# Three-pass mixer projections in layer 0 of a two-block network, and token tiles summed, scaled and turned in two halves between its expert layers

## The chip, the cores and the metric

The kernel runs on one core of a Trainium2 chip. The metric is the time of one execution on the device in microseconds, the median of several runs.

The engines of the core are named as the profile names them. PE is TensorE (matmuls), and PEld its weight loads. DVE is VectorE, ACT is ScalarE, POOL is GpSimd. SP issues most DMAs. Each engine works through its own queue in order, and the kernel orders the engines among each other by semaphores written out by hand.

## The reference

Two blocks of two layers each follow one another on 256 tokens of width 1024. The first block (an mLSTM and neighbourhood attention, then a differential attention, each with memory attention and a gated feed-forward part) is not touched by the change except at its seam with the second block. The second block is:

```python
def layer(x, xc, ..., need_ctx):
    h = rms_norm_2(x, n1) * (1 + sc1) + sh1
    hc = rms_norm_2(xc, n1) * (1 + csc1) + csh1
    a_b, a_c, a_h, b_v, b_g, c_q, c_k, c_v, d_q, d_k, d_v = split_proj(h @ w_in)
    ca_b, ca_c, ca_h, ... , cd_v = split_proj(hc @ w_in)
    ya = short_conv_mixer(a_b, a_c, a_h, conv_a)
    yb = conformer_conv(b_v, b_g, conv_b, ...)          # 31 taps over the tokens
    yc = window_attention(apply_rope(c_q), apply_rope(c_k), c_v, ...)
    yd = global_attention(apply_rope(rms(d_q)), apply_rope(rms(d_k)), d_v, ...)
    x_new = x + g1 * (concatenate([ya, yb, yc, yd]) @ w_out)
    h2 = rms_norm_2(x_new, n2) * (1 + sc2) + sh2
    x_new = x_new + g2 * expert_choice_ffn(h2, router, w_gate, w_up, w_down)
    ...                                                 # the same for xc where need_ctx
```

In layer 0 the 256 tokens x and the 256 context tokens xc both go through all of it; in layer 1 only x does, and xc gives keys and values alone. Each layer has 16 experts with three matrices of 1024x1024 in float32, all of which are read from HBM: some 200 MB per layer.

## The kernel before, in words

**Stages.** The first block takes the first 1020 us or so. Then come, for layer 0 of the second block: the projections by `w_in` (columns in five blocks, in the order b, d, c, ab, ah of `IN2_BLOCKS`), the 31-tap convolution and the norms and rotations of queries and keys beside them, the attention of 16 units, the output projection by `w_out`, the routing, and the experts in 8 groups of two. Layer 1 follows with the same stages for half the tokens, with 4 groups of four experts.

**Two ways to multiply.** In the first block the weights are *split*: ACT rounds a unit (128 partitions x 4 chunks x 512 columns, 1 MB) into one of four slots for high parts (`split_through`, L1733), POOL subtracts that from the whole unit in place, chunk by chunk, which leaves the low part (L1638, `w_lo`), and PE multiplies in three passes, high by high, low by high and high by low (`passes`, L624 to L626), with both operands as fp32r. A high slot is free again when PE has read the unit four before it; POOL walks through all the units in one loop (L1630 and after), in which a few waits, `yields`, are written in. In the second block the operands are plain float32, and each float32 matmul stands in the trace as two records. The `w_in` units of the second block are loaded straight into slots of the ring of 12.

**Layer 0, projections.** PE first multiplies the context half of the four outputs of block b (L1149), while DVE finishes the last norm of the first block, then turns the token rows (L1165), then multiplies the token half. ACT and DVE share the evacuation of the turned rows, which scales and shifts them (L2124, L2750). Blocks d and c have two outputs of queries (L1198, by halves of 64 columns), one of keys (L1189) and one of values, made with the tokens in the partitions (L1206). Block ab has four outputs and ah two (L1189). The ah outputs are computed behind the first two units of the attention.

**Beside them.** DVE computes the gate of the convolution (L2766), then its 31 taps for two channel halves (L2771, L2773: 60 operations of one tap), then root and rotation of queries and keys (L2794, L2800, L2802, L2781 to L2784), then the norm of the convolution's rows (L2810 to L2819), then the maxima of the attention (L2385 to L2398). PE waits for it at the rotation of dk0 (L1224), before the first scores (L824) and at each turning of probabilities (L836). POOL computes gate diagonals and small tables (L1667 to L1691) and is then idle until the short convolution (L1699).

**Between the layers.** The last group's outputs are scattered by 8 matmuls into 8 banks (L1451) and added to x by DVE (L2964) in the order of `sums_of`, in which context and token tiles alternate. ACT squares each tile (L2091), DVE scales it (L2957), and PE turns all four tiles (L1177) before the first output of block b.

**DMA.** SP issues the loads in the order of use. Each waits until the slot it overwrites has been read. The first 19 quarter matrices of layer 0's experts have homes of their own; the rest follow in the ring as PE reads it.

Of the kernel before, what the change touches and what calls it, by code (L numbers as in the profile page):

```python
# [219 lines left out]
def build(nc, w, out, table, stop=None):  # L220
    marks = Marks(table)
    units = weight_plan(w)
    first2 = [key[0] for key, _ in units].index("in2")
# [21 lines left out]
    with ExitStack() as ctx:  # L245
# [69 lines left out]
        x_lo, m_lo = xT_r[:, :, 0:SEQ], xT_r[:, :, SEQ:2 * SEQ]  # L315
        y1_lo = x_r[:, 2:4, :].rearrange("p a (b c) -> p (a b) c", c=SEQ)
# [77 lines left out]
        last_sum_banks = (6, 7, 0, 1, 2, 3, 4, 5)  # L394
# [165 lines left out]
        QK_AT = dict(cq0=0, cq1=1, ck0=2, dq0=4, dq1=5, dk0=6)  # L560
        ROT_BANK = dict(cq0=6, cq1=7, ck0=6, dq0=7, dq1=4, dk0=5)
# [9 lines left out]
        def _(pe):  # L571
# [544 lines left out]
            for layer in range(DEPTH):  # L1116
# [27 lines left out]
                def chunk_half(name, b, wb, at, s, first):  # L1144

                    for c in range(KC):
                        if not first and name == "bv0" and c % 2 == 0:
                            pe.wait_ge(*after("hT_odd" if c // 2 % 2 else "hT", (layer, 0, c // 2)))
                        mm = pe.matmul(b[:, SEQ * s:SEQ * s + SEQ], wb(c)[:, at:at + P], xT[:, c, SEQ * s:SEQ * s + SEQ],  # L1149
                                       start=(first and c == 0), stop=(not first and c == KC - 1))  # L1150
                    return mm

                if layer == 0:
                    wb0 = w_block(("in2", layer, "b"))
                    early = [(name, at, open_bank(("c", layer, name), 4 + i)) for i, (name, at) in enumerate((k, v) for k, v in CHUNKS.items() if k[0] == "b")]
                    pe.wait_ge(*after("hT_odd", "ctx"))
                    for name, at, b in early:
                        chunk_half(name, b, wb0, at - IN2_BLOCKS[0][1], 1, True)
                    for t in range(T2):
                        pe.wait_ge(*after("xhat", (layer, 0, t)))  # L1160
                    for j in range(4):
                        b = dense_bank(("h", layer, 0, j))
                        for c in (2 * j, 2 * j + 1):
                            for t in range(T2):
                                mm = pe.transpose(b[:, 256 * (c % 2) + P * t:256 * (c % 2) + P * t + P], xhat[:, t, P * c:P * c + P], ident)  # L1165
                        mm.then_inc(*filled_now(("h", layer, 0, j)))
                    for name, at, b in early:
                        chunk_half(name, b, wb0, at - IN2_BLOCKS[0][1], 0, False)\
                            .then_inc(bank_full[fills[("c", layer, name)][0]], 1)
                        last_fill[0] = full(("c", layer, name))  # L1170
                else:
                    for t in range(4):
                        pe.wait_ge(*after("xhat", (layer, 0, t)))
                    for c in range(KC):
                        b = dense_bank(("h", layer, 0, c))
                        for t in range(4):
                            mm = pe.transpose(b[:, P * t:P * t + P], xhat[:, t, P * c:P * c + P], ident)  # L1177
                        mm.then_inc(*filled_now(("h", layer, 0, c)))
                def chunk_there(c):

                    pe.wait_ge(*after("hT_odd" if c % 2 else "hT", (layer, 0, c)))

                def chunk(name, wb, at, n=n_tok):
                    key = ("c", layer, name)
                    b = open_bank(key, LATE_BANK[name]) if name in LATE_BANK else dense_bank(key)
                    for c in range(KC):
                        if layer and name == "bv0":
                            chunk_there(c)
                        mm = pe.matmul(b[:, 0:n], wb(c)[:, at:at + P], xT[:, c, 0:n], start=(c == 0), stop=(c == KC - 1))  # L1189
                    mm.then_inc(*filled_now(("c", layer, name)))  # L1190

                def queries(name, wb, j):

                    b = dense_bank(("c", layer, name))
                    for c in range(KC):
                        for v in range(2):
                            at = HD * (2 * v + j)
                            mm = pe.matmul(b[HD * v:HD * v + HD, 0:n_tok], wb(c)[:, at:at + HD], xT[:, c, 0:n_tok],  # L1198
                                           start=(c == 0), stop=(c == KC - 1))
                    mm.then_inc(*filled_now(("c", layer, name)))  # L1200

                def values2(name, wb, at):
# [5 lines left out]
                    mm.then_inc(*filled_now(("c", layer, name)))  # L1208

# [29 lines left out]
                for blk, n0, n1 in IN2_BLOCKS:  # L1239
                    wb = wb0 if (layer, blk) == (0, "b") else w_block(("in2", layer, blk))  # L1240
                    if blk in "dc":
                        for i in range(2):
                            queries(f"{blk}q{i}", wb, i)
                        if blk == "c":
                            square_sums2(("dq0", "dq1"))
                        chunk(blk + "k0", wb, 2 * P, 2 * SEQ)
                        values2(blk + "v", wb, 3 * P)
                        if blk == "c":
                            square_sums2(("dk0",))
                            rotations(("cq0", "cq1"))  # L1250
                        if blk == "d":
# [10 lines left out]
                            mm.then_inc(*filled_now(("refold", layer)))  # L1262
# [1857 lines left out]
```

## Time and profile before

| | |
|---|---|
| median of 3 runs | 2422.28 us (2420.02 to 2424.28) |
| the profiled execution | 2422.65 us, its span on the core 2420.8 us |
| PE busy | 2184.5 us (90%) |
| PEld busy | 1350.8 us |
| DVE busy | 752.7 us |
| ACT busy | 633.9 us |
| POOL busy | 740.4 us |
| mean granted TensorE clock | 0.961 of full speed |
| HBM read | 633.17 MB |

The shares of the whole span hide that the stages differ. The first block and layer 0's mixer are full of PE work; the expert stages run at 407 to 428 GB/s of DMA. The change touches the stretch from about 1020 us to 1310 us (layer 0 without its experts) and the seam at 1765 us to 1860 us, so the profile is to be read there.

### The profile page before, as it was taken

The numbers are of one execution on the slowest core, as the hardware profiler recorded it, in microseconds if no ns is written. First come the engines' busy times: TensorE is split into PE (matmuls) and PEld (weight loads), VectorE is DVE, ScalarE is ACT, GpSimd is POOL, SyncE is SP. The second block draws the span as 40 slices with busy tenths as digits, with TensorE's granted clock in tenths as the row PEclk, the third lists the DMA queues.
The fourth block names the chain that finished last, engine by engine and source line by source line (L and its number), as shares of the span: only waits on it lengthen the run. The fifth ranks groups of instructions, "written<-read, shape, count | busy, mean of one in ns | idle before, by whom it ended". The sixth has DMA issues, their size and how long they took to land.

```text
span 2420.8 us, 32870 instructions
## 1 busy us (share of the span) xinstructions
PE 2184.5 (90%) x13382; PEld 1350.8 (56%) x13382; DVE 752.7 (31%) x1440; ACT 633.9 (26%) x925; POOL 740.4 (31%) x624
## 2 busy tenths in 40 slices
PE   7998999999799999999999999999889995888885
PEld 7876789878687898865543333333257642222221
DVE  4864220122622212377623222222147420010101
ACT  3544333444544334112512000010022420000001
POOL 7665367897183777710300000000010200000000
PEclk9999999999899999999999999999999998999998
DMA  9433759755157697441215899999962369999997
GB/s 299 140 120 125 261 198 325 236 183 174 36 187 252 209 324 238 149 173 38 84 52 209 347 428 428 429 429 429 423 226 83 127 279 424 427 428 428 429 428 306
DMA packets 151381, 635.98 MB, mean 263 GB/s; under 512 B 7816, under 2 KB 14216, under 8 KB 120920
## 3 DMA queue, kind: packets, MB, share of 16 engines
q1 hardware_dynamic: 148224, 623.78, 66.3%
q0 software_dynamic: 2608, 9.25, 1.4%
q8 instruction: 86, 1.41, 0.2%
q10 hardware_dynamic: 424, 1.22, 0.1%
q14 instruction: 39, 0.32, 0.0%
HBM read 633.17 MB, written 1.05 MB: 262 GB/s over the span
## 4 chain that ended last, share of the span: by engine, by line
PE 65%; DMA 19%; DVE 7%; POOL 4%; ACT 2%; issue 2%; SPq 1%; DVEq 0%; ACTq 0%; POOLq 0%
PE bank L1374 14%; PE bank L624 9%; PE bank L626 9%; PE bank L625 9%; DMA ring<-in_w_gate 8%; DMA ring<-in_w_up 7%; DMA ring<-in_w_down 4%; PE bank L1189 4%; PE bank L1332 3%; POOL ring_r L1638 2%; PE bank L847 2%; PE bank L970 2%; PE bank L1198 2%; PE bank L824 1%; PE bank L1206 1%
## 5 line engine op out<-in xcount | busy, mean ns | idle before, releaser
L1374 PE MATMUL bank<-ring,arena 128*32 128x512 f32 x4424 | 651.5, 625 | 127.0 <-DMA ring<-in_w_gate 54.6
L1638 POOL TENSOR_TENSOR ring_r<-ring,ring_r 128x512 fp32r<-128x512 f32 (+1 forms) x468 | 574.9, 1270 | 294.1 <-ACT ring_r L1733 265.1
L1374 PEld LDWEIGHTS bank<-ring,arena 128*32 128x32 f32 x4424 | 191.5, 114 | 562.3 <-issue 536.4
L624 PE MATMUL bank<-ring_r 128*128 128x256 f32 (+1 forms) x1504 | 463.5, 308 | 13.0 <-POOL ring_r L1638 7.8
L626 PE MATMUL bank<-xT_r,ring_r 128*128 128x256 f32 x1248 | 354.3, 284 | 0.0
L625 PE MATMUL bank<-ring_r 128*128 128x256 f32 x1104 | 312.4, 283 | 0.0
L624 PEld LDWEIGHTS bank<-ring_r 128*128 128x128 f32 x1504 | 289.3, 192 | 35.9 <-issue 16.7
L1733 ACT ACTIVATE ring_r<-ring 128x2048 fp32r<-128x2048 f32 (+1 forms) x119 | 216.7, 1827 | 288.7 <-DMA ring<-in_ffn_w_gu 139.9
L626 PEld LDWEIGHTS bank<-xT_r,ring_r 128*128 128x128 f32 x1248 | 239.6, 192 | 0.0
L625 PEld LDWEIGHTS bank<-ring_r 128*128 128x128 f32 x1104 | 211.6, 192 | 0.7 <-issue 0.5
L1667 POOL TENSOR_TENSOR arena<-const 128x1024 f32<-128x1024 f32 x6 | 12.0, 2002 | 592.0 <-DVEq L2284 522.6
L1765 ACT ACTIVATE arena<-bank 128x512 f32<-128x512 f32 (+1 forms) x144 | 83.6, 581 | 257.1 <-PE bank L836 72.0
L2252 ACT ACTIVATE arena<-bank 128x512 f32<-128x512 f32 x24 | 13.0, 594 | 486.6 <-PE bank L1374 486.6
L2964 DVE TENSOR_TENSOR x<-x,bank 128x512 f32<-128x512 f32 x80 | 52.0, 684 | 218.3 <-PE bank L1451 217.7
L1189 PE MATMUL bank<-xT,ring 128*128 128x512 f32 (+1 forms) x320 | 110.7, 504 | 1.9 <-ACTq L2200 1.9
L1638 POOL TENSOR_TENSOR spare_r<-spare,ring_r 128x512 fp32r<-128x512 f32 x76 | 100.5, 1360 | 12.0 <-ACT ring_r L1733 7.2
L1189 PEld LDWEIGHTS bank<-xT,ring 128*128 128x128 f32 x320 | 63.0, 199 | 44.7 <-issue 37.1
L2939 DVE TENSOR_TENSOR arena<-bank,arena 128x512 f32<-128x512 f32 x24 | 15.5, 686 | 232.6 <-PE bank L1374 232.6
L626 PE MATMUL bank<-ring_r 128*128 128x512 f32 x208 | 84.3, 405 | 0.0
L624 PE MATMUL bank<-ring_r,arena_r 128*128 128x512 f32 (+1 forms) x208 | 79.3, 381 | 2.2 <-POOL ring_r L1638 2.0
L1699 POOL TENSOR_TENSOR arena<-arena 128x512 f32<-128x512 f32 (+1 forms) x4 | 3.8, 950 | 250.6 <-ACTq L1771 250.4
L625 PE MATMUL bank<-ring_r,arena_r 128*128 128x512 f32 (+1 forms) x208 | 78.5, 378 | 0.0
(358 smaller groups left out, 2719.6 us busy)
## 6 DMA issues: line engine op xcount, KB each, us to landing
ring<-in_w_gate SPq DMA_DIRECT2D x52, 2048.0 KB, 17.3
ring<-in_w_up SPq DMA_DIRECT2D x52, 2048.0 KB, 17.3
ring<-in_w_down SPq DMA_DIRECT2D x40, 2048.0 KB, 18.2
ring<-in_ada_w SPq DMA_DIRECT2D x41, 1024.0 KB, 7.5
ring<-in_w_down SPq DMA_DIRECT2D x41, 1024.0 KB, 18.4
ring<-in_ffn_w_gu SPq DMA_DIRECT2D x35, 1024.0 KB, 5.7
ring<-in_w_up SPq DMA_DIRECT2D x18, 1024.0 KB, 8.7
ring<-in_w_gate SPq DMA_DIRECT2D x17, 1024.0 KB, 5.0
```

Source lines behind the costliest of these rows:

```text
L624: pe.matmul(dst, w_hi, v_hi, start=first, stop=False)
L625: pe.matmul(dst, w_lo, v_hi, start=False, stop=False)
L626: return pe.matmul(dst, w_hi, v_lo, start=False, stop=last)
L847: mm = pe.matmul(b[p0:p0 + dv, 256 * i:256 * i + 256], u["v"][kb][:, i * dv:(i + 1) * dv], probsT_of(u)[:, kb, :], start=(kb == 0), stop=( ...
L970: mm = pe.matmul(b[32 * j:32 * j + 32, :], scT[:, UK * h + k, :], ws[j][:, k], start=(h == 0 and k == 0), stop=(h == 1 and k == UK - 1))
L1189: mm = pe.matmul(b[:, 0:n], wb(c)[:, at:at + P], xT[:, c, 0:n], start=(c == 0), stop=(c == KC - 1))
L1332: mm = pe.matmul(b[:, :], src[:, t * P:t * P + P], wb(c), start=(c == 0), stop=(c == KC - 1))
L1374: mm = pe.matmul(dst[nb][CAP * b:CAP * b + CAP, :], src[:, c, CAP * b:CAP * b + CAP], rooms[b % G], start=bi_first, stop=bi_last)
L1638: pool.tensor_tensor(lo[:, c], whole[:, c], hi_of(u)[:, c, 0:n], ALU.subtract).then_inc(*signal("w_lo", (u, c)))
L1733: act.activation(hi_of(u)[:, 0:kc, 0:n_col], room_of(slot)[:, 0:kc, 0:n_col], ACT.Copy).then_inc(*signal("w_hi", u))
L1765: link(act.activation(dst, src, func))
L2964: dve.tensor_tensor(xs, xs, bank[bank_at][:, :], ALU.add).then_inc(m["sum_free"], 1)
```

## The change

- The `w_in` units of layer 0 join the split units: they are loaded into the slots of raw units, rounded by ACT and subtracted by POOL. The ring begins with the `w_out` units of layer 0, whose first two slots hold the high parts of the layer's input (`h_hi`) until block ah has been multiplied.
- The input of layer 0's projections is split too. DVE scales the turned context in PSUM, copies the high part and subtracts the low part; for the tokens ACT writes the high part, and DVE scales in PSUM and subtracts.
- All outputs of blocks b, d, c, ab, ah of layer 0 are made by three passes (`split_chunk`). The values are made turned, like the others, and then turned back by PE (`turn_values`). The queries' columns are put in order when the inputs are prepared, so that one output has 128 columns, in both layers.
- ACT's splits for block d stand after the norm's root, for c after the sigmoids, for ab after the evacuation of dv, for ah after that of cv. POOL does block b's subtractions before, and the other eight units' after, its small tables.
- Between the layers the two token tiles are summed, scaled and turned first (`turn_hidden(0)`), and the two context tiles follow (`turn_hidden(1)`, before block d). The banks of the last sums change.

```diff
-    first2 = [key[0] for key, _ in units].index("in2")
+    first2 = [key[0] for key, _ in units].index("out2")
...
+        h_hi, h_lo = ring_r[:, MEM_HI:X_HI + 1].rearrange("p s a b -> p (s a b)").rearrange("p (c n) -> p c n", c=KC), xT_r
...
-        last_sum_banks = (6, 7, 0, 1, 2, 3, 4, 5)
+        last_sum_banks = (0, 4, 1, 5, 2, 6, 3, 7)
...
+                def split_chunk(name, wb, at, wait=False):
+
+                    key = ("c", layer, name)
+                    b = open_bank(key, LATE_BANK[name]) if name in LATE_BANK else dense_bank(key)
                     for c in range(KC):
+                        mm = passes(b[:, :], wb(c, at, wait), (h_hi[:, c], h_lo[:, c]), c == 0, c == KC - 1)
+                    mm.then_inc(*filled_now(key))
...
+                    turn_hidden(0)
+                    for c in range(KC):
+                        if c % 2 == 0:
+                            pe.wait_ge(*after("hT_odd", (layer, 0, c // 2)))
+                        for name, at, b in early:
+                            mm = passes(b[:, 0:SEQ], wb0(c, at - IN2_BLOCKS[0][1], False), (h_hi[:, c, 0:SEQ], h_lo[:, c, 0:SEQ]), False, c == KC - 1)
...
+                def turn_values(name):
+
+                    pe.wait_ge(*after("proj", ("vT", name)))
+                    b = dense_bank(("vt", name))
+                    for t in range(4):
+                        mm = pe.transpose(b[:, P * t:P * t + P], qk[:, VT_AT[name], P * t:P * t + P], ident)
+                    mm.then_inc(*filled_now(("vt", name)))
...
                         if blk == "c":
                             square_sums2(("dk0",))
                             rotations(("cq0", "cq1"))
+                            if layer == 0:
+                                turn_values("cv")
...
+            in2_at = place[unit_at[("in2", 0, "b", 0)]]
+            lows(0, in2_at + 2)
...
                 ins.then_inc(*signal("spread", layer))
+                if layer == 0:
+                    lows(in2_at + 2, len(split_units))
...
                     norm_rows(0, range(T2))
+                    split_through(place[unit_at[("in2", 0, "d", 1)]])
...
+                if layer == 0:
+                    split_through(place[unit_at[("in2", 0, "c", 1)]])
...
-                evac(("c", layer, "dv"), v2[:, :, 1, :])
+                values_in("dv")
+                if layer == 0:
+                    split_through(place[unit_at[("in2", 0, "ab", 1)]])
...
-                evac(("c", layer, "cv"), v2[:, :, 0, :])
+                values_in("cv")
+                if layer == 0:
+                    split_through(place[unit_at[("in2", 0, "ah", 1)]])
+                roots(("dk0",))
...
-                        mean_of(ready[1])
-                        scaled_rows(ready[0])
-                        mean_of(ready[2])
-                        scaled_rows(ready[1])
-                        mean_of(ready[3])
-                        scaled_rows(ready[2])
-                        scaled_rows(ready[3])
+                        mean_of(0)
+                        add_half(2, 0)
+                        mean_of(1)
+                        scaled_rows(0)
+                        scaled_rows(1)
+                        add_half(2, 1)
+                        for nb in range(2):
+                            add_half(3, nb)
+                        mean_of(2)
+                        mean_of(3)
+                        scaled_rows(2)
+                        scaled_rows(3)
```

## Rows read from the trace of the kernel before

**Rows 1.** Stages: us, busy time (instructions) of PE, PEld, DVE, ACT, POOL, clock, DMA

```profile
1050.00:1100.00 50.00, 50.00 (x237) 23.76 (x234) 46.90 (x63) 9.58 (x18) 0.00 (x0) 1.00 0.24 85
1151.00:1223.00 72.00, 68.18 (x296) 40.01 (x294) 44.56 (x120) 39.64 (x96) 20.03 (x14) 1.00 0.17 65
1309.00:1765.00 456.00, 422.90 (x3440) 139.74 (x3444) 89.86 (x171) 39.56 (x62) 0.00 (x0) 0.97 0.96 407
```

**Rows 2.** Timeline of PE in layer 0: start us, us, engine, line, operation, count

```profile
1019.90 13.97 PE L1149 MATMUL bank<-xT,ring 128*128 128x256 f32 x64
1033.71 1.91 PE L1165 MATMUL bank<-const,arena 128*128 128x128 f32 x16
1098.09 7.03 PE L1189 MATMUL bank<-xT,ring 128*128 128x512 f32 x16
1130.25 3.72 PE L824 MATMUL bank<-arena 64*128 64x256 f32 x16
1150.62 1.09 PE L836 MATMUL bank<-const,arena 128*128 128x128 f32 x8
```

**Rows 3.** Timeline of PE, three-pass products of the first block, 512 and 256 wide

```profile
984.33 0.40 PE L626 MATMUL bank<-ring_r,arena_r 128*128 128x512 f32 x1
985.03 0.40 PE L626 MATMUL bank<-ring_r,arena_r 128*128 128x512 f32 x1
...
904.81 0.28 PE L624 MATMUL bank<-ring_r 128*128 128x256 f32 x1
905.16 0.28 PE L624 MATMUL bank<-ring_r 128*128 128x256 f32 x1
```

**Rows 4.** Timeline of DVE in layer 0

```profile
1015.98 0.70 DVE L2322 SCALAR_TENSOR_TENSOR bank<-x,bank 128x512 f32<-128x512 f32 x1 [20.41 <-PE bank L626]
1029.42 2.73 DVE L2732 TENSOR_SCALAR arena<-x,rstd 128x1024 f32<-128x1024 f32 x2
1051.38 0.55 DVE L2771 TENSOR_SCALAR arena<-arena,cols 128x512 f32<-128x512 f32 x1 [0.15 <-DVE arena L2766]
1076.29 23.59 DVE L2773 SCALAR_TENSOR_TENSOR arena<-arena,cols 128x512 f32<-128x512 f32 x30
1127.69 0.42 DVE L2784 TENSOR_TENSOR arena<-arena 128x256 f32<-128x256 f32 x1
1142.70 0.88 DVE L2408 TENSOR_SCALAR arena<-arena,small 128x512 f32<-128x512 f32 x2
```

**Rows 5.** Timeline of ACT and POOL: splitting, the turned tokens, a table load

```profile
994.90 1.92 ACT L1733 ACTIVATE ring_r<-ring 128x2048 fp32r<-128x2048 f32 x1 [5.02 <-PE bank L626]
...
992.21 17.54 POOL L1638 TENSOR_TENSOR ring_r<-ring,ring_r 128x512 fp32r<-128x512 f32 x14
...
1034.41 1.02 ACT L2124 ACTIVATE xT<-bank,const,gain 128x256 f32<-128x256 f32 x2 [5.23 <-PE bank L1165]
1043.58 1.28 ACT L2135 ACT_TABLE_LOAD   x1 [0.17 <-ACT arena L1765]
```

**Rows 6.** First block, DVE beside POOL: a group of 41:54 us, then timeline rows

```profile
L2493 DVE SCALAR_TENSOR_TENSOR arena<-arena,cols 128x256 f32<-128x256 f32 x1 | 14.5, 14516 | 0.0
...
...
78.11 1.64 DVE L2474 TENSOR_TENSOR arena<-arena,x 4x512 f32<-4x512 f32 x1
74.48 6.68 POOL L1638 TENSOR_TENSOR ring_r<-ring,ring_r 128x512 fp32r<-128x512 f32 x4
```

**Rows 7.** Timeline of SP's loads for layer 0's experts

```profile
1171.79 0.43 SPq L1527 DMA_DIRECT2D spare<-in_w_down  x1
1230.15 0.33 SPq L1527 DMA_DIRECT2D arena<-in_w_gate  x1
```

**Rows 8.** Timeline of PE at the seam and in layer 1

```profile
1780.14 6.30 PE L1177 MATMUL bank<-const,arena 128*128 128x128 f32 x32 [8.68 <-DVE arena L2957]
...
1847.50 3.62 PE L1189 MATMUL bank<-xT,ring 128*128 128x256 f32 x16
1856.55 5.30 PE L1189 MATMUL bank<-xT,ring 128*128 128x256 f32 x16
```

More of the change, by code:

```diff
@@ L1142, in gate_slots, with split_block, chunk_of @@
                             keep_busy(2)
-                def chunk_half(name, b, wb, at, s, first):
-                    for c in range(KC):
[L1147 to L1151, printed above, removed]
+                def split_block(key):
+                    parts = [split_weights(key, h) for h in range(2)]
+                    def chunk_of(c, at, wait):
+                        u, hi, lo = parts[c // UK]
+                        if wait:
+                            chunk_split(u, c % UK)
+                        return hi[:, c % UK, at:at + P], lo[:, c % UK, at:at + P]
+                    return chunk_of
@@ L1183, in chunk, with chunk_there @@
+                    read(("in2", layer, "b"), 2)
+                else:
+                    turn_hidden(0)
+                def chunk_there(c, s):
+                    if c % 2 == 0:
+                        pe.wait_ge(*after("hT_odd" if c // 2 % 2 else "hT", (layer, s, c // 2)))
                 def chunk(name, wb, at, n=n_tok):
@@ L1186, in chunk @@
                     for c in range(KC):
-                        if layer and name == "bv0":
-                            chunk_there(c)
+                        if layer and name in ("bv0", "dk0"):
+                            chunk_there(c, 1 if name == "dk0" else 0)
                         mm = pe.matmul(b[:, 0:n], wb(c)[:, at:at + P], xT[:, c, 0:n], start=(c == 0), stop=(c == KC - 1))
[L1190 to L1199, printed above, removed]
                     mm.then_inc(*filled_now(("c", layer, name)))
@@ L1262, in _ @@
                             mm.then_inc(*filled_now(("refold", layer)))
+                            if layer == 0:
+                                turn_values("dv")
                     elif blk == "ab":
-                        chunk("ab0", wb, 0)
+                        gated = chunk if layer else split_chunk
+                        if layer:
+                            chunk("ab0", wb, 0)
+                        else:
+                            split_chunk("ab0", wb, 0, wait=True)
                         rotations(("ck0", "dq0", "dq1"))
@@ L1272, in _ @@
                             scores(u)
[L1273 to L1275 removed]
+                        gated("ac0", wb, 2 * P)
+                        gated("ac1", wb, 3 * P)
+                        read(("in2", layer, "ab"), 2)
+                    elif blk == "b":
                         for name, at in CHUNKS.items():
@@ L1648, in _, with lows @@
                         .then_inc(*signal("lam_in", 0, 16))
+            def lows(first, last):
+                for i in range(first, last):
+                    low_parts(i, split_units[i])
+            in2_at = place[unit_at[("in2", 0, "b", 0)]]
+            lows(0, in2_at + 2)
             if stop:
@@ L2045, in _ @@
                 else:
-                    roots(n0 + 2, follow_blocks(("down", layer, 0), ("down", layer, 1)))
+                    roots(n0 + 2, lambda short: split_through(place[unit_at[("in2", 0, "b", 1)]]))
             if stop:
```

186 lines of the change are left out of this document (107 added, 79 removed).

## The prediction

> **What bounds the kernel now.** I read the table of stages first, because the shares of the whole span mix stages with different limits. From 1050 to 1100 us, in the mixer of layer 0, PE is busy all the time and DVE for 46.9 of the 50 us, while POOL does nothing [rows 1]. The reader should see two engines side by side there, of which only PE is quite full. From 1309 us the experts run at 407 GB/s [rows 1]: that stage is bound by its DMA stream, and the stream flows as PE empties the homes. So whatever PE gains or loses ahead of 1309 us moves the whole stage by as much. Then I read the timelines of PE and DVE in layer 0, to see who would be next if PE were faster, and last a place in the first block where DVE and POOL work at once.
>
> The sum is made against the profiled execution, 2422.65 us with 1.85 us of it outside the span, which is 0.4 us above the median of 2422.28.
>
> **What PE saves.** A float32 output of 512 columns over eight chunks takes 7.03 us [rows 2]. Three passes of 512 columns take 0.70 us per chunk (985.03 minus 984.33) [rows 3], so 5.6 us for eight: 1.4 us less. I take queries and values at the same. Of the sixteen such outputs in blocks d, c, ab (twelve), and b (four), b is made in halves of 256: its context half takes 13.97 us now [rows 2], and 32 chunks x 0.35 us (905.16 minus 904.81) = 11.2 us then [rows 3]. Block ah has two more outputs. So d, c and ab save 17, ah 2.8 and b 5.6 us, together some 25.5 us. The two turnings of values take 8 records each, half of L1165's 1.91 us for 16 [rows 2], 1.9 us together. PE's own work shrinks by 23.6 us. That would be the gain if nothing else were close.
>
> **What DVE allows.** Its convolution runs from 1051.38 to 1099.88 (the second thirty taps start at 1076.29 and last 23.59), the last rotation ends at 1128.1, and the first probabilities are ready at 1143.6 [rows 4]. PE starts the first scores at 1130.25 and turns the first probabilities at 1150.62 [rows 2]. So PE's slack against DVE is only 2.1 us at the scores and 7.0 us at the turning, and most of PE's gain before that is worth nothing unless the convolution starts earlier.
>
> When does it start? Now the token rows are scaled at 1032.15 [rows 4], but PE is in the context half until 1033.7 and then turns [rows 2]. After, that half takes 2.8 us less, and PE turns at 1032.3. Then comes a new chain: ACT writes the high part of two chunks, 1.0 us [rows 5]; DVE scales them again in PSUM, about the same, and subtracts, 0.7 us by its like row of 512 elements [rows 4]; with what lies between, some 4 us to the first product at 1036.3. All four outputs then grow together and end at 1047.5, 2.1 us sooner than by now's times, but all at once: four evacuations and the table load of 1.28 us [rows 5], some 4.5 us, stand in a row behind them instead of beside PE. The convolution starts at about 1052.1, 0.7 us later; I hold this to 1 us either way.
>
> **What POOL does to DVE.** This is the largest term. The change queues eight units on POOL behind its small tables, four subtractions each. One takes 1.25 us alone (17.54 us for 14), and ACT's rounding 1.92 us per unit [rows 5]. Units d0 and d1 are done by 1047, before the convolution. Units c0 and c1 are rounded after the sigmoids (from 1051) and ab0, ab1 after block d (from 1071): 16 subtractions fall into the convolution, whose taps read two operands in SBUF. In the first block the trace shows what that does. A tap of 256 elements took 14.5 us while POOL's subtractions ran through [rows 6]. An operation of 512 elements took 1.64 us while POOL's four took 6.68, 1.67 each [rows 6]: here the two take turns. A tap takes 0.786 us now (23.59 over 30) [rows 4]. In turns, a tap and a subtraction take some 1.70 us together, so each subtraction costs DVE 0.91 us, and sixteen cost 14.6 us. The bounds are 0 (if such a tap isn't held up after all) and 16 x 1.25 = 20 us (if DVE is shut out, as in the row of 14.5 us). I take 14.6 by the row of 512 elements, which is the tap's size. The convolution ends at 1099.9 + 0.7 + 14.6 = 1115.2.
>
> The Trainium skill, "SBUF — State Buffer", in its section on the ports says that a DVE operation with two SBUF inputs and a GpSimd operation that reads SBUF exclude each other for a whole instruction. It speaks against this change. The trace agrees in kind [rows 6]; by that rule alone no tap would pass beside a subtraction, which is rival C at worst and the forecast at best.
>
> **From the convolution's end to the first turning of probabilities.** That is 50.7 us now (1099.9 to 1150.62), PE being late; DVE's own chain needs 43.7 (to 1143.6). After, ACT's roots of dq0 and dq1 wait for DVE and stand ahead of the evacuations of ck0 and cv and of the rounding of ah, so POOL subtracts ah's eight chunks from 6 to about 18 us behind the convolution's end. DVE meets them with five operations on SBUF: at 0.91 us 4.5 us, bounds 0 and 10 (eight times 1.25). So 48.2 us in place of 50.7. PE stands idle meanwhile: it is through block c at about 1103 and waits for a bank that DVE frees at 1116, and again for dk0's norm. Behind an idle stretch in layer 1, 16 records took 5.30 us where they had taken 3.62 [rows 8]. So I charge 2 us for a lower clock, bounds 0 and 5. Block ah stands inside the attention, where PE is busy 68.2 of 72 us [rows 1], so its 2.8 us count in full.
>
> Sum for layer 0: 0.7 + 14.6 - 2.5 + 2.0 - 2.8 = 12.0 us later.
>
> **Moved at no cost, and the cover.** DVE's extra work on the context (four copies and four subtractions, some 7 us) stands in a wait of 20.41 us that ends at 1015.98 [rows 4]. Block b must be split by 1019.90 [rows 2]: PE's last two units of the product before take 12 chunks x 0.70 = 8.4 us, so the slots come free at 1005.9 and 1011.5; ACT rounds in 1.92 us, POOL is through its queue at 1009.75 and takes 10 us more [rows 5], just in time. If that cover fails, PE waits for a unit's 5 us less what DVE's norm hides. All loads of output weights and experts now wait for ah's second output, since the input's high parts lie in the first ring slots. SP then issues 13 MB, 34 us at 407 GB/s [rows 1]; now SP has 58 us there without a load (1171.79 to 1230.15) [rows 7]. Without that gap each MB would cost 2.6 us.
>
> **The seam.** PE is idle for 8.68 us and then turns 32 records in 6.30 us [rows 8]. After, the first two tiles are summed, squared and scaled some 4 us earlier, and 16 records are turned. But DVE scales the other two tiles before its share of the evacuation, so the first output is held up and ends 3.0 us earlier only. The other 16 records (1.9 us) come before block d, whose first output waits for a bank. PE keeps 0.9 us, the convolution 0.5. I take 0.8, bounds -1 (a loss) and 3.
>
> **Sum.** 12.0 - 0.8 = 11.2 us longer: 2433.9 for the profiled execution, 2433.5 beside the median.
>
> **Rivals.**
> - A, turns are taken, as above: 2433.5, its own range 2426 to 2440 (tail 0 to 10 us, clock 0 to 5, seam -1 to 3).
> - B, DVE isn't held up: neither the 14.6 nor the 4.5 nor the 2.0 us are paid, 21.1 us less than A, so 9.9 us faster, 2412.4. For it: no tap of 512 elements on 128 partitions stands beside POOL in the trace. Against it: the rows of 14.5 and 1.64 us [rows 6]. Between A and B it turns at (9.9 - 2.0) over 21 operations: below 0.38 us per subtraction the kernel isn't slower.
> - C, DVE is shut out while POOL streams: 20 and 10 us in place of 14.6 and 4.5, 11 us more than A, 2444.
> - D, subtractions and taps meet in part only, or some slip by: 5 to 10 of the 16 are free, 4.5 to 9 us less than A and some of the tail, 2422 to 2428.
> - E, the change does on the clock what it does on PE: all 23.6 us arrive, and the seam's 0.8, 2398. The convolution would have to start far earlier, which rows 4 exclude.
>
> **How the numbers follow.** Chances: A 0.50, C 0.10, D 0.14, B 0.22, E 0.04. A measurement of this kernel can tell about 0.2% (4.8 us) from no change. Slower by more than that are A, C and a little of D, 0.62; within it most of D, 0.13; faster B and E, 0.25. The range goes from B's time to A's upper end and a little beyond, 2411 to 2441. The likeliest case alone: 2426 to 2440.
>
> **What would show it.** Right: taps of about 1.7 us wherever POOL subtracts, and a convolution that ends about 15 us later; PE idle ahead of dk0's square sums and ahead of its rotation, released by DVE; outputs of 5.6 us. Wrong: taps that stay at 0.75 us beside POOL (B), one tap of 5 to 10 us (C), PE waiting for low parts or for output weights (a cover gone). At the seam PE should turn some 4 us sooner after the last scatter.

## The result, and the profile after

| | before | changed |
|---|---|---|
| median of 20 runs each | 2423.54 us (2414.97 to 2427.59) | 2432.75 us (2420.89 to 2449.53) |
| ratio changed / before | | 1.0038, 95% interval 1.0025 to 1.0051 |
| profiled execution | 2422.65 us, span 2420.8 | 2435.95 us, span 2434.2 |

The changed kernel is slower by 9.2 us by the medians; the interval of the ratio says 6 to 12. The forecast was 2433.5, 11.2 us more than before. The medians and ratios below leave out one execution of quarter_c_ab_later that took 3032.52 us, far above its eleven others.

Where does it come from? First the convolution of layer 0 on DVE, then POOL beside it (the timelines of the kernel after; start, duration, engine, line, operation, tiles). L2848 is the first of the 31 taps of a channel half, L2850 the other thirty, L1678 the subtractions, L2879 the scaling by the root, L2877 the reciprocal.

```profile
1054.41 0.55 DVE L2848 TENSOR_SCALAR arena<-arena,cols 128x512 f32<-128x512 f32 x1 [0.15 <-DVE arena L2841]
1054.99 38.09 DVE L2850 SCALAR_TENSOR_TENSOR arena<-arena,cols 128x512 f32<-128x512 f32 x30
1093.23 0.55 DVE L2848 TENSOR_SCALAR arena<-arena,cols 128x512 f32<-128x512 f32 x1 [0.15 <-DVE arena L2850]
1093.81 23.59 DVE L2850 SCALAR_TENSOR_TENSOR arena<-arena,cols 128x512 f32<-128x512 f32 x30
1119.49 3.35 DVE L2877 RECIPROCAL arena<-arena 128x512 f32<-128x512 f32 x1 [0.24 <-DVE arena L2871]
1122.88 1.12 DVE L2879 SCALAR_TENSOR_TENSOR arena<-arena,cols 128x512 f32<-128x512 f32 x1
1136.65 0.75 DVE L2879 SCALAR_TENSOR_TENSOR arena<-arena,cols 128x512 f32<-128x512 f32 x1
```

```profile
1055.45 13.36 POOL L1678 TENSOR_TENSOR ring_r<-ring,ring_r 128x512 fp32r<-128x512 f32 x8 [8.68 <-ACT ring_r L1781]
1075.21 13.39 POOL L1678 TENSOR_TENSOR ring_r<-ring,ring_r 128x512 fp32r<-128x512 f32 x8 [6.39 <-ACT ring_r L1781]
1122.72 3.27 POOL L1678 TENSOR_TENSOR ring_r<-ring,ring_r 128x256 fp32r<-128x256 f32 x4 [34.12 <-ACT ring_r L1781]
1125.94 3.28 POOL L1678 TENSOR_TENSOR spare_r<-spare,ring_r 128x256 fp32r<-128x256 f32 x4
```

All sixteen subtractions fall into the first thirty taps, which take 38.09 us in place of 23.59; the second thirty, with POOL idle beside them, take 23.59 as before. A subtraction takes 1.67 us there (13.36 over 8). The convolution ends at 1117.4.

Next PE behind it, in the timeline of the same kernel (the bracket is its idle time ahead of a row, and what ended it).

```profile
1118.52 2.05 PE L1234 MATMUL bank<-arena,const 128*128 128x512 f32 x2 [10.70 <-DVEq L2356]
1137.52 1.22 PE L1241 MATMUL bank<-arena,const 128*128 128x256 f32 x2 [3.35 <-DVEq L2353]
1145.14 3.72 PE L826 MATMUL bank<-arena 64*128 64x256 f32 x16
1162.91 1.10 PE L838 MATMUL bank<-const,arena 128*128 128x128 f32 x8
1233.02 1.55 PE L1371 MATMUL bank<-ring,arena 128*128 128x512 f32 x3 [0.68 <-DVEq L2353]
```

The reader should see PE with nothing to do for 10.7 us ahead of dk0's square sums (L1234) and for 3.35 us ahead of its rotation (L1241, the last one), both times released by DVE; before, it was busy there without a gap. Scores (L826) start 14.9 us later than in [rows 2], the first turning of probabilities (L838) 12.3 us later, the output projection (L1371) 10.0 us later than in this row of before:

```profile
1222.98 3.70 PE L1332 MATMUL bank<-ring,arena 128*128 128x512 f32 x8 [0.68 <-DVEq L2284]
```

The table of stages, of after (the stretches that answer to [rows 1]):

```profile
1055.00:1105.00 50.00, 47.13 (x188) 36.37 (x187) 48.29 (x46) 15.53 (x22) 26.75 (x16) 0.93 0.06 17
1105.00:1163.00 58.00, 41.60 (x168) 31.43 (x167) 47.00 (x77) 15.72 (x28) 6.50 (x8) 0.85 0.00 1
1319.00:1775.00 456.00, 422.22 (x3436) 131.69 (x3440) 89.77 (x171) 39.57 (x62) 0.00 (x0) 0.97 0.96 406
```

PE and DVE have changed places: DVE is the full one, and from 1105 PE works 41.6 of 58 us at a granted clock of 0.85. The experts run at 406 GB/s, as before.

**A mark against drift.** Up to PE's turning of the context's chunks both kernels do the same, and still one profiled execution is there sooner than the other:

```profile
987.36 1.91 PE L1106 MATMUL bank<-const,xT 128*128 128x128 f32 x16
988.31 1.91 PE L1108 MATMUL bank<-const,xT 128*128 128x128 f32 x16
```

In the ten other profiles of this study the same step starts between 983.50 and 994.36. So below I count times from this step, and give each as its difference to the kernel before (us, from the timelines; the first tap is the tensor_scalar ahead of the thirty, and the last column is where the last run of expert products begins):

| kernel | first tap | convolution ends | output projection, layer 0 | last scatter, layer 0 | first tap, layer 1 | last expert products |
|---|---|---|---|---|---|---|
| changed | +2.1 | +16.6 | +9.1 | +9.5 | +8.6 | +8.5 |
| seam_only | 0.0 | 0.0 | 0.0 | +0.3 | -0.7 | -0.9 |
| layer0_only | +0.5 | +15.0 | +7.2 | +1.7 | +1.2 | -3.8 |
| thin_subs | +0.5 | +0.6 | -7.4 | -6.9 | -7.8 | -8.2 |
| half_subs | +2.1 | +13.3 | +5.8 | +6.0 | +5.1 | +5.0 |
| quarter_subs | +0.5 | +5.2 | -2.2 | -2.2 | -3.7 | -4.4 |
| ab_after_conv | +0.5 | +7.8 | +1.6 | +2.1 | +1.2 | +1.0 |
| quarter_c_ab_later | +0.5 | +3.0 | -2.0 | +0.2 | -0.7 | -1.2 |
| gates_first | +0.5 | +3.0 | -4.0 | -3.7 | -4.6 | -4.8 |
| few_taps_before | 0.0 | -44.1 | 0.0 | -2.3 | -2.9 | -1.9 |
| few_taps_after | +0.5 | -40.1 | -12.4 | -10.5 | -11.3 | -13.0 |

The last column isn't yet the end. These rows are the last expert products and the last scatters, first of before, then of the changed kernel:

```profile
2405.10 1.92 PE L1374 MATMUL bank<-ring,arena 128*32 128x512 f32 x16 [2.35 <-DMA ring<-in_w_down]
2408.51 3.67 PE L1451 MATMUL bank<-arena 128*128 128x512 f32 x8 [1.49 <-DVE arena L2939]
```

```profile
2414.59 3.64 PE L1413 MATMUL bank<-ring,arena 128*32 128x512 f32 x16 [3.09 <-DMA ring<-in_w_down]
2419.72 5.78 PE L1490 MATMUL bank<-arena 128*128 128x512 f32 x8 [1.49 <-DVE arena L3016]
```

The changed kernel's profiled execution loses another 3.8 us there: the granted clock is 0.57 from 2412.2 to 2424.2, where before has 0.95 from 2398.8 to 2410.8. So its span ends 12.4 us later by the mark, and not 8.5. Six other kernels, few_taps_before among them, wait 3.1 us for the same load and need 3.3 us for these products, but their scatters take 3.67; scatters of 5.7 us stand in few_taps_after alone. I don't count the 3.8 us as an effect of the change; that it is none is not shown.

### The profile page after: what moved, and what is told of

Its sections match the earlier page's. It is cut to its first block, busy times and chain, and to the rows that moved or that the text cites. A ratio compares the mean times of both kernels' runs of the same rounds, so it can differ in the third digit from the quotient of the medians.

```text
span 2434.2 us, 32873 instructions
## 1 busy us (share of the span) xinstructions
PE 2180.8 (90%) x13342; PEld 1371.7 (56%) x13342; DVE 778.9 (32%) x1456; ACT 653.7 (27%) x941; POOL 792.5 (33%) x664
## 4 chain that ended last, share of the span: by engine, by line
PE 61%; DMA 19%; DVE 11%; ACT 3%; POOL 3%; issue 2%; SPq 1%; DVEq 0%; ACTq 0%; POOLq 0%
PE bank L1413 15%; PE bank L626 10%; PE bank L628 9%; PE bank L627 9%; DMA ring<-in_w_gate 9%; DMA ring<-in_w_up 7%; PE bank L1371 3%; DMA ring<-in_w_down 3%; DVE arena L2850 2%; PE bank L1208 2%; PE bank L849 2%; PE bank L972 2%; POOL ring_r L1678 2%; PE bank L826 1%; PE bank L1490 1%
## 5 line engine op out<-in xcount | busy, mean ns | idle before, releaser
L1678 POOL TENSOR_TENSOR ring_r<-ring,ring_r 128x512 fp32r<-128x512 f32 (+1 forms) x500 | 620.1, 1284 | 344.2 <-ACT ring_r L1781 315.5
L626 PE MATMUL bank<-ring_r 128*128 128x256 f32 (+1 forms) x1680 | 528.5, 315 | 16.8 <-POOL ring_r L1678 8.2
L628 PE MATMUL bank<-xT_r,ring_r 128*128 128x256 f32 (+1 forms) x1424 | 418.4, 294 | 0.0
L627 PE MATMUL bank<-ring_r 128*128 128x256 f32 (+1 forms) x1256 | 367.0, 292 | 0.0
L626 PEld LDWEIGHTS bank<-ring_r 128*128 128x128 f32 x1680 | 323.5, 193 | 46.4 <-issue 19.2
L1781 ACT ACTIVATE ring_r<-ring 128x2048 fp32r<-128x2048 f32 (+1 forms) x127 | 230.8, 1825 | 298.3 <-DMA ring<-in_ffn_w_gu 141.8
L628 PEld LDWEIGHTS bank<-xT_r,ring_r 128*128 128x128 f32 x1424 | 274.4, 193 | 5.1
L627 PEld LDWEIGHTS bank<-ring_r 128*128 128x128 f32 x1256 | 241.7, 192 | 5.1 <-issue 0.7
L1678 POOL TENSOR_TENSOR spare_r<-spare,ring_r 128x512 fp32r<-128x512 f32 (+1 forms) x84 | 108.7, 1332 | 12.0 <-ACT ring_r L1781 7.3
L2850 DVE SCALAR_TENSOR_TENSOR arena<-arena,cols 128x512 f32<-128x512 f32 (+1 forms) x120 | 88.7, 739 | 4.3
L2993 DVE TENSOR_TENSOR arena<-posT,const 128x128 f32<-128x128 f32 (+1 forms) x20 | 6.3, 316 | 224.0 <-PE bank L1500 223.5
L849 PE MATMUL bank<-arena 128*64 128x256 f32 (+1 forms) x272 | 69.2, 392 | 7.6 <-DVEq L2356 7.6
## 6 DMA issues: line engine op xcount, KB each, us to landing
ring<-in_w_up SPq DMA_DIRECT2D x18, 1024.0 KB, 11.2
```

The lines of the kernel that those rows point to most:

```text
L626: pe.matmul(dst, w_hi, v_hi, start=first, stop=False)
L627: pe.matmul(dst, w_lo, v_hi, start=False, stop=False)
L628: return pe.matmul(dst, w_hi, v_lo, start=False, stop=last)
L849: mm = pe.matmul(b[p0:p0 + dv, 256 * i:256 * i + 256], u["v"][kb][:, i * dv:(i + 1) * dv], probsT_of(u)[:, kb, :], start=(kb == 0), stop=( ...
L1678: pool.tensor_tensor(lo[:, c], whole[:, c], hi_of(u)[:, c, 0:n], ALU.subtract).then_inc(*signal("w_lo", (u, c)))
L1781: act.activation(hi_of(u)[:, 0:kc, 0:n_col], room_of(slot)[:, 0:kc, 0:n_col], ACT.Copy).then_inc(*signal("w_hi", u))
```

## The experiments

My theory after the result: DVE pays for POOL's subtractions beside its taps, and PE, with little slack against DVE, ends up waiting. The rivals: the loss sits elsewhere (the late start, the seam, the clock), or PE saves less than I worked out. Each ratio below is to executions of the kernel before that were taken in the same rounds; their medians are 2424.73 us for seam_only, layer0_only, thin_subs and half_subs, 2424.05 for the few taps, quarter_subs and ab_after_conv, and 2425.25 for the last two.

**1. The two halves of the change apart.** seam_only is the kernel before with

```
-        last_sum_banks = (6, 7, 0, 1, 2, 3, 4, 5)
+        last_sum_banks = (0, 4, 1, 5, 2, 6, 3, 7)
...
+                    turn_hidden(0)
...
+                        if layer and blk == "d":
+                            turn_hidden(1)
```

and what belongs to it on ScalarE and DVE; layer0_only is the changed kernel with these undone.

> Only the second half of the change: between the expert layers the token tiles are summed in order of tile, scaled and turned first; layer 0 is the kernel before's, float32 products and all. My theory: the scatter to the first product of block b falls from 18.5 us to about 12.5, but d begins only some 1.6 us sooner and the convolution of layer 1 0.9 us sooner, so 1 to 3 us of the total go: 2420.5 to 2422.5. Rival: DVE holds everything behind, nothing is left at the end, 2423 to 2424.

> Only the first half of the change: layer 0's projections in three passes with POOL's subtractions; the step between the expert layers is the kernel before's. My theory: the first turning of probabilities comes 12 us later and so does the end, 2434 to 2436, which is the changed kernel's 2432.8 plus what the other half saves. Rival: the loss is in the other half, then this one is at 2424 or less.

Measured: seam_only 2423.22 us, ratio 0.9986 (0.9968 to 1.0005); layer0_only 2433.03 us, ratio 1.0030 (1.0011 to 1.0049). The loss is all in layer 0. Both medians lie up to 1 us outside what I expected: seam_only's at its rival's 2423 to 2424, though 1.5 us under the kernel before of its rounds, and layer0_only's 1.0 below. The other half is worth 0.9 us in its trace and cannot be told from nothing by time. Its parts in seam_only: the first product of block b comes sooner, but DVE's first tap in layer 1 only 0.7 us; the output projection comes 2.3 us sooner; and where the experts of layer 1 start 0.8 us are left. In layer0_only's profiled execution the expert stage of layer 0 took 453.0 us, where it took 458.5 to 459.1 in nine others (456.9 in quarter_subs, 454.6 in few_taps_before); that is why its last columns are early. What shortened it I don't know, and its median does not show it. At the output projection it is 1.9 us ahead of the changed kernel, which has the same layer 0: 1.5 us stand at the first tap, where the granted clock differs (see the next section), and 0.4 behind the convolution.

**2. The subtractions taken away.** thin_subs is the changed kernel with, for c and ab,

```
+                n_sub = 1 if i in thin else n
                 for c in range(kc):
-                    pool.tensor_tensor(lo[:, c], whole[:, c], hi_of(u)[:, c, 0:n], ALU.subtract).then_inc(*signal("w_lo", (u, c)))
+                    pool.tensor_tensor(lo[:, c, 0:n_sub], whole[:, c, 0:n_sub], hi_of(u)[:, c, 0:n_sub], ALU.subtract).then_inc(*signal("w_lo", (u, c)))
```

and the high part read in the second pass too.

> The changed kernel, but for blocks c and ab POOL subtracts one column in place of 512, and TensorE's second pass reads the high part of the weights again in place of the low part (this leaves out the low parts of those two blocks; waits, passes and rounding stay as many). My theory: the sixteen subtractions cost the convolution 14.5 us, so its taps are back at 0.79 us and it ends near 1103. PE had 10.7 us of waiting there, so PE becomes the bound for the rest: 10 to 12 us of the total go, 2421 to 2423. Rival: the convolution is late for another reason (its start, the clock) and the time stays above 2430.

Measured: 2416.87 us, ratio 0.9974 (0.9962 to 0.9987), 15.9 us under the changed kernel. Its DVE timeline:

```profile
1050.43 23.61 DVE L2854 SCALAR_TENSOR_TENSOR arena<-arena,cols 128x512 f32<-128x512 f32 x30
1074.77 23.59 DVE L2854 SCALAR_TENSOR_TENSOR arena<-arena,cols 128x512 f32<-128x512 f32 x30
```

The taps are back at 0.79 us, and the whole 14.5 us come off the convolution (48.5 us from its first tap, 63.0 in the changed kernel). This is the proof of the term. My second sentence there was wrong: PE does not become the bound for the rest. It goes straight on from block c at 1102.65, but then waits for DVE all the same (3.35 us ahead of the last rotation), and only behind that rotation is it busy without a pause; so more came back than the 10 to 12 us expected. With the contention gone three passes would be a gain of 6 to 8 us over the kernel before.

**3. The same elements in smaller pieces.** half_subs makes each of the sixteen as two of 256 columns, quarter_subs as four of 128:

```
+                        for k in range(0, n, 128):
+                            ins = pool.tensor_tensor(lo[:, c, k:k + 128], whole[:, c, k:k + 128], hi_of(u)[:, c, k:k + 128], ALU.subtract)
```

> The changed kernel with each subtraction of blocks c and ab (128x512) made as two of 128x256: 32 operations in place of 16, the same elements. Theory one: a tap and a subtraction overlap by the fixed part of each (0.786 plus 1.25 alone, 1.67 to 1.70 together, so 0.34 us), and a subtraction half as wide takes some 0.66 alone: each then costs 0.32, 32 of them 10 us in place of 14.5, the time falls by 4 us to about 2429. Theory two: it is the elements that cost, the same 14.5 us, 2433. Theory three: each change of turn costs 0.91 whatever the width, 29 us, and the time rises by 12 or more.

> The changed kernel with each subtraction of blocks c and ab made as four of 128x128: 64 operations, the same elements. Halves gave a tap and a subtraction 1.145 us together, 0.36 over the tap's 0.786; whole ones 0.89. A 128x128 operation of POOL takes 0.40 alone in its small tables. Theory one (cost is the subtraction's own time less 0.34 us that overlap): 0.06 each, 4 us in all, the convolution ends near 1107 and the time falls to 2421 to 2425, unless PE waits for low parts that now come one in 0.85 us. Theory two (every change of turn costs at least the 0.36 of the halves): 64 x 0.36 = 23 us over whatever part of them meets the taps, slower than the changed kernel, over 2438.

Measured: half_subs 2431.38 us, ratio 1.0024 (1.0007 to 1.0041); quarter_subs 2426.11 us, ratio 1.0002 (0.9981 to 1.0024). From quarter_subs, DVE and then POOL:

```profile
1057.96 25.88 DVE L2856 SCALAR_TENSOR_TENSOR arena<-arena,cols 128x512 f32<-128x512 f32 x30
1084.58 25.99 DVE L2856 SCALAR_TENSOR_TENSOR arena<-arena,cols 128x512 f32<-128x512 f32 x30
```

```profile
L1681 POOL TENSOR_TENSOR ring_r<-ring,ring_r 128x128 fp32r<-128x128 f32 x64 | 53.7, 875 | 7.1 <-ACT ring_r L1787 7.1
```

From the first tap to the convolution's end it takes 48.5 us without subtractions, 63.0 with sixteen whole ones, 59.7 with 32 halves, 53.2 with 64 quarters: 0.91, 0.35 and 0.07 us for each. Theory one of both runs held for the convolution: what a subtraction costs DVE is its own time alone (1.25 us, some 0.70 from start to start at that width in the first block of before, 0.40) less some 0.34 us that the two overlap. Both times came out above what I expected from it (2429, and 2421 to 2425), by 2.4 and 1.1 us, less than the intervals are wide. The price is not one of elements nor of turns alone. POOL pays instead: it needs 53.7 us of operations for what took it 26.8, since only one piece fits beside each tap.

**4. The subtractions moved past the convolution.** ab_after_conv adds one wait on POOL:

```
+            yields[place[unit_at[("in2", 0, "ab", 0)]]] = ("uconv", (0, 1))
```

> The changed kernel with one wait more: POOL starts block ab's eight subtractions when the convolution is done. My theory: eight at 0.89 us leave the convolution, which ends 7 us sooner; PE reads the first low part of ab some 6 us after the convolution's end and gets one chunk in 1.25 us, so it loses 2 to 4 us, and DVE's tail meets some of them; 3 to 6 us go, 2427 to 2430. Rival: the tail is so tight that all of it comes back, 2432 to 2435.

Measured: 2424.93 us, ratio 0.9995 (0.9981 to 1.0009), 7.8 us under the changed kernel, more than the 3 to 6 I expected. Rows of its DVE timeline:

```profile
1055.83 30.91 DVE L2851 SCALAR_TENSOR_TENSOR arena<-arena,cols 128x512 f32<-128x512 f32 x30
...
1112.22 0.69 DVE L2872 TENSOR_SCALAR arena<-bank 128x512 f32<-128x512 f32 x1 [0.24 <-DVE arena L2872]
...
1116.54 1.42 DVE L2880 SCALAR_TENSOR_TENSOR arena<-arena,cols 128x512 f32<-128x512 f32 x1
1118.11 3.35 DVE L2878 RECIPROCAL arena<-arena 128x512 f32<-128x512 f32 x1
...
1123.88 0.72 DVE L2862 TENSOR_TENSOR arena<-arena 128x256 f32<-128x256 f32 x1
```

Eight subtractions beside the taps cost 7.3 us (30.91 less 23.59), 0.91 each again. The other eight run from 1111.20 beside DVE's tail, and cost it little: the reciprocal keeps its 3.35 us, an operation on a bank its 0.69, and only the few with two operands in SBUF are held (1.42 in place of 0.75, 0.72 in place of 0.42). From the convolution's end to the first turning it takes 46.7 us, where the changed kernel takes 45.5. PE waited for a low part once, 0.27 us.

**5. What PE's gain is worth when DVE is out of the way.** few_taps_before and few_taps_after are the two kernels with

```
-                    for j in range(1, CONV_B):
+                    for j in range(1, CONV_B if layer else 3):
```

> The kernel before, with 3 of the 31 taps of layer 0's convolution (this leaves out 28 taps of each half, 44 us of DVE's work). My theory: PE was the bound there, DVE two microseconds behind it, so the time stays at 2423, give or take 1.5. Rival: DVE set the end, and up to 44 us go.

> The changed kernel, with 3 of the 31 taps of layer 0's convolution (28 taps of each half are left out, as in the other one). My theory: with DVE out of the way what PE saves arrives: 23.6 us less 1 to 3 us for the later first output, and the step between the expert layers 1 to 3 us: 19 to 25 us under the kernel before with few taps, 2398 to 2404. Rival: the three passes save less than 1.4 us an output, or the loss lies elsewhere than at the convolution: less than 10 us under it.

Measured: few_taps_before 2422.88 us, ratio 0.9994 (0.9979 to 1.0009); few_taps_after 2415.71 us, ratio 0.9959 (0.9940 to 0.9977). The first held: 44 us less of DVE's work change nothing, so PE was the bound. The second missed: 7.2 us by the medians, and in the traces 12.4 at the output projection, where I had 19 to 25 for the whole; the rival had said less than 10. At the last expert products the two traces are 11.1 us apart. Two places took most of the rest. Block d starts only 2.3 us sooner: b's context half is 2.8 us faster, but PE then stands 0.96 and 1.78 us ahead of the turned rows and of the first product. And behind block d:

```profile
1071.76 3.60 PE L1129 MATMUL bank<-arena,const 128*128 128x512 f32 x8
1078.22 1.84 PE L1289 MATMUL bank<-col,arena 128*128 128x8 f32 x8 [2.87 <-ACTq L1814]
```

```profile
1072.80 3.71 ACT L1781 ACTIVATE ring_r<-ring 128x2048 fp32r<-128x2048 f32 x2 [0.25 <-ACT arena L1813]
1076.42 1.13 ACT L2206 ACTIVATE arena<-arena 128x512 f32<-128x512 f32 x2
1077.46 2.72 ACT L1813 ACTIVATE arena<-bank 128x512 f32<-128x512 f32 x4
```

ScalarE rounds block ab ahead of the gate rows, PE waits 2.87 us for their bank, and comes back at half speed. The windows of the same kernel, ahead of it and behind it (the seventh number from the left without those in brackets, 1.00 and 0.50, is the granted clock):

```profile
1071.00:1078.00 7.00, 4.35 (x12) 1.91 (x11) 0.00 (x0) 5.79 (x6) 3.21 (x3) 1.00 0.27 75
1078.00:1084.00 6.00, 5.78 (x22) 5.33 (x23) 0.00 (x0) 2.77 (x8) 6.00 (x6) 0.50 0.01 3
```

A clock of 0.50 is the 1.2 GHz level. L1289 took 0.95 us before and 1.84 here; the first output of block c took 7.3 us, the others 5.7. So PE, 8.0 us ahead of before at the end of block d, is 3.0 ahead at the start of block c. Two smaller waits follow, 0.89 us for DVE ahead of the last rotation and 1.26 for ScalarE ahead of ah's first output. The changed kernel has the wait of 2.87 us at L1289 too; there it is hidden, since PE waits for DVE later anyway.

**6. The remedies together.** quarter_c_ab_later joins quarters in block c to ab's later start; gates_first puts ScalarE's rounding of ab behind the gate rows as well:

```
                 values_in("dv")
-                if layer == 0:
-                    split_through(place[unit_at[("in2", 0, "ab", 1)]])
...
                     evac(("vt", "dv"), v2[:, :, 1, :])
+                    split_through(place[unit_at[("in2", 0, "ab", 1)]])
```

> Both remedies at once: block c's eight subtractions made as 32 of 128x128, block ab's eight whole ones started when the convolution is done. My theory: the 32 cost DVE 2.4 us (0.07 each), the convolution ends 5 us sooner than with whole ones in c, which is when PE is through block c, so DVE and PE meet there and PE keeps 3 to 5 us of it: the output projection of layer 0 starts 2 to 4 us sooner than in the kernel before, counted from the turning of the context, and the time is 2417 to 2422. Rival: PE, waiting for ab's low parts at one in 1.25 us, and DVE's tail eat it, 2424 to 2427.

> The one above, and ScalarE rounds block ab behind the gate rows in place of ahead of them. With few taps PE waited 2.87 us for ScalarE at the refold products, and then ran 2 to 3 us behind at half clock. My theory: that wait goes, PE is through block c 3 to 6 us sooner, but DVE's convolution ends only where it did, so at most 1 us of the total goes: 2417 to 2421, the same as the one above within a microsecond or so. Rival: PE was the later one there, and 3 to 6 us go.

Measured: quarter_c_ab_later 2422.49 us, ratio 0.9982 (0.9963 to 1.0001); gates_first 2421.89 us, ratio 0.9983 (0.9960 to 1.0005). In both the convolution ends 3.0 us later than in the kernel before. In gates_first the wait for ScalarE is gone, PE is through block c sooner, and then waits for DVE:

```profile
1109.47 1.19 PE L1234 MATMUL bank<-arena,const 128*128 128x512 f32 x1 [4.24 <-DVEq L2362]
```

Both are level with the kernel before or a little under it, and 10 us under the changed one; neither interval excludes 1. Both medians lie just above what I expected. Between the two the times tell nothing, and the traces 2 us at the output projection, where I had expected 1 at most. Of these 1.4 us are the clock: behind the last rotation quarter_c_ab_later is granted 0.50 for 4.5 us and its next output takes 8.4 us, gates_first 0.67 and 7.0.

## Why the prediction was right, and where it was not

- **The subtractions beside the taps: right, and it is the cause.** Forecast 16 x 0.91 = 14.6 us; the trace has 38.09 - 23.59 = 14.50, and all of it comes off when the sixteen are made thin. The rows that carried it were the first block's 1.64 and 1.67 us [rows 6]. Rivals B (none), C (20 us) and D (some slip by) fall. The Trainium skill, "SBUF — State Buffer", in its section on SBUF's two sides, has the two exclude each other "for the whole instruction". The traces agree in kind and in which operations are held; by size each pair overlaps 0.34 us.
- **The start of the convolution: right.** Forecast 0.7 us later, 1 either way. It is 0.5 in seven kernels with three passes, and 2.1 in the changed one and in half_subs, where the first output of block b ran partly at half clock (0.57 granted from 1038 to 1042; its 24 records 4.5 us, elsewhere 3.1).

```profile
1038.00:1042.00 4.00, 4.00 (x24) 4.00 (x23) 3.43 (x7) 0.00 (x0) 4.00 (x5) 0.57 0.00 0
```

- **From the convolution's end to the first turning: too dear.** Forecast 48.2 us and 2.0 for the clock, measured 45.5 with the clock in it. Two steps failed. One is the price of ah's eight subtractions, 4.5 us: units of ah are only 256 wide, and a subtraction of 256 columns costs 0.35, not 0.91. They met two operations that were held, 0.37 and 0.35 us, 0.7 together. The other is that DVE's own chain was taken at 43.7 us, and these held a wait for PE. The first row is of before, the second of the changed kernel:

```profile
1113.59 0.42 DVE L2781 TENSOR_TENSOR arena<-bank,const 128x256 f32<-128x256 f32 x1 [3.20 <-PE bank L1224]
```

```profile
1157.88 0.89 DVE L2477 TENSOR_SCALAR arena<-arena,small 128x512 f32<-128x512 f32 x2
```

The wait of 3.20 us is gone after the change, so DVE has the probabilities ready 41.4 us behind the convolution's end (1158.8). PE, busy without a pause from its last rotation at 1137.52, turns them only at 1162.91: behind that rotation PE is the later one again, as before the change.
- **The lower clock: about right.** Charged 2 us on that path. Most of the half clock falls where DVE is late anyway, but behind the last rotation it is on the path. The changed kernel first, then layer0_only, whose layer 0 is the same (the granted clock is again the seventh number):

```profile
1137.50:1142.00 4.50, 4.48 (x13) 3.64 (x14) 3.57 (x10) 0.00 (x0) 0.00 (x0) 0.66 0.00 0
```

```profile
1139.90:1144.40 4.50, 4.50 (x20) 3.71 (x21) 3.61 (x10) 0.00 (x0) 0.00 (x0) 1.00 0.00 0
```

At a granted clock of 0.66 the next output takes 7.0 us, at 1.00 it takes 5.9, and from the convolution's end to the first turning layer0_only needs 44.0 us in place of 45.5. So the clock cost 1.5 us there.
- **Block ah: nearly right.** Forecast -2.8, measured -2.2: first turning to output projection 70.1 us, before 72.4.
- **Sum for layer 0.** Forecast 12.0; with the mark 9.1. The stretch behind the convolution was put 4.7 us too high, the start 1.4 too low (the half clock at the first output) and the gain of ah 0.6 too high. That these partly cancel is luck.
- **The covers: held.** PE waits for no low part of b; POOL takes 5.00 us for each of d's units and is done before the convolution. SP goes from 1191.38 to 1240.18 without a load, in the place of [rows 7], so the transfers held back until ah's second output had room.
- **The seam: right by the traces.** Forecast -0.8; seam_only's trace has -0.9, the changed kernel's -0.6 (8.5 at the last expert products less 9.1 at layer 0's output projection). The medians cannot tell it from nothing. In the changed kernel PE's first product comes 12.5 us behind the scatter's start (1790.64 less 1778.17), before 18.5 (1786.27 less 1767.75), so the first output gains more than the 3.0 us forecast. But block b is through only 3.5 us sooner, the other sixteen turnings (1.9 us) follow, so d has 1.6 and the convolution 0.9.
- **What PE saves: wrong, and hidden.** The outputs do take 5.6 us. That the 23.6 us "would be the gain if nothing else were close" is not right: without DVE's taps in the way 12.4 arrive at the output projection. I had not looked at ScalarE, whose rounding of ab stands ahead of the gate rows. Rival E at 2398 could not have come even with the convolution out of the way. What could have been had without contention is thin_subs, 6.3 us under the kernel before by the ratio, 7.9 by the medians, not the 9.9 of rival B.
- **The total.** Forecast +11.2, measured +9.2 by the medians, and by the mark +8.5 at the last expert products and +12.4 at the end of the profiled span. The largest term, 14.6, is the one that was shown; that the total is within 2 us owes something to errors that cancel.

## What to carry to other kernels

A saving on the engine that is full is worth only the slack of the one behind it, and the slack must be read against every engine that the change loads, ScalarE's order of work too. A chain of the engine behind, read from the trace before, must be read without its own waits for the engine that gets faster. Where GpSimd has to work on SBUF beside DVE operations that read two SBUF tensors, put its work beside reciprocals, operations on PSUM or waits, or cut it into pieces of 128 columns if its result isn't urgent. Compare traces from the last step that is the same in both kernels.

## What the runs showed of the hardware

- POOL subtractions (two operands and result in SBUF) beside DVE taps (128x512, two operands in SBUF, 0.786 us): 0.91 us for each of 512 columns, 0.35 for 256, 0.07 for 128, nothing that can be seen for 1. The pair takes 1.67, 1.15 and 0.85 us.
- DVE operations with one operand in SBUF (reciprocal, 3.35 us) or one in PSUM (0.69 us) keep their time while POOL streams.
- An idle stretch of PE of only 1.8 to 2.9 us was followed by half clock, at b's first output in two of nine kernels with three passes and behind the wait for ScalarE in few_taps_after; an idle stretch of the same length at b's first output left the clock alone in the other seven. Ahead of the last rotation 2.00 us of idle were followed by 0.50 in quarter_c_ab_later, and 2.04 us by 1.00 in layer0_only. What tells them apart stays open.
- The same program code reaches the same step at 983.5 to 994.4 us in different executions. Where in the first 983 us that comes from was not looked into; it makes single profiles unfit for differences under some 10 us unless they are counted from a common step.
